# Weights in their second role: the values' halves stored 32 bytes further into their slots

## What is computed

```python
h = rmsnorm(x, g_pre)
u = h @ w_in                        # queries, keys, values, gates of three branches
o_a = latent attention              # first branch, 8 heads
o_b = differential attention        # second branch, 8 heads of value width 128
o_c = banded attention with bias    # third branch, 8 heads of value width 128
y = sum over n of gate_n * ((o_n * silu(z_n)) @ w_branch[n])
x = x + y @ w_out
```

## Time and profile before

| | |
|---|---|
| median of 3 runs | 3364.19 us (3363.44 to 3365.39) |
| the profiled execution's own time | 3364.12 us |
| its span (first to last instruction) | 3362.4 us |
| PE busy | 3319.8 us, 99% of the span |
| DVE busy | 2190.8 us, 65% |
| ACT busy | 1714.9 us, 51% |
| mean granted PE clock | 0.998 of full |

### The profile page before, as it was taken

One profiled execution on the slowest core, in us unless ns is written; L12 is line 12 of the kernel. 1 busy time (PEld: TensorE's weight loads), 2 busy tenths in 40 slices (PEclk: granted clock), 3 DMA queues, 4 the chain that ended last, 5 costly groups with the idle time before them and its releaser, 6 DMA issues. The chain is left out here.

```text
span 3362.4 us, 72952 instructions
## 1 busy us (share of the span) xinstructions
PE 3319.8 (99%) x27834; PEld 3279.7 (98%) x27834; DVE 2190.8 (65%) x3584; ACT 1714.9 (51%) x2803; POOL 309.7 (9%) x314
## 2 busy tenths in 40 slices
PE   7999999999999999999999999999999999999999
PEld 7999999999999999899999999999899999999999
DVE  7667666656656666678755665665778755666655
ACT  5555644434434455656544554444665654554443
POOL 1010100000000025011002200001012101210000
PEclk9999999999999999999999999999999999999999
DMA  5334455555555554344455545554444455445554
GB/s 187 109 112 148 176 185 190 188 187 186 190 186 188 186 189 163 135 163 163 156 203 184 180 163 188 187 198 177 148 151 164 155 178 206 173 163 188 188 206 163
DMA packets 90629, 584.28 MB, mean 174 GB/s; under 512 B 10480, under 2 KB 11120, under 8 KB 28400
## 3 DMA queue, kind: packets, MB, share of 16 engines
q1 hardware_dynamic: 88992, 577.47, 48.6%
q0 software_dynamic: 1488, 4.72, 0.4%
HBM read 580.05 MB, written 2.10 MB: 173 GB/s over the span
## 5 line engine op out<-in xcount | busy, mean ns | idle before, releaser
L174 DVE TENSOR_TENSOR w_lo<-raw,w_hi 128x768 fp32r<-128x768 f32 (+5 forms) x1202 | 1378.7, 1159 | 372.3 <-ACT w_hi L163 365.0
L193 PE MATMUL bank<-h,w_hi 128*128 128x256 f32 x5168 | 1459.2, 282 | 17.2 <-DVE w_lo L174 12.7
L163 ACT ACTIVATE w_hi<-raw 128x768 fp32r<-128x768 f32 (+4 forms) x1190 | 1096.8, 969 | 689.8 <-PE bank L195 614.6
L195 PE MATMUL bank<-h,w_lo 128*128 128x256 f32 x5168 | 1443.7, 279 | 0.0
L194 PE MATMUL bank<-h,w_hi 128*128 128x256 f32 x5168 | 1443.4, 279 | 0.0
L193 PEld LDWEIGHTS bank<-h,w_hi 128*128 128x128 f32 x5168 | 972.7, 188 | 22.8 <-DVE w_lo L174 10.8
L194 PEld LDWEIGHTS bank<-h,w_hi 128*128 128x128 f32 x5168 | 972.9, 188 | 2.6 <-issue 1.9
L195 PEld LDWEIGHTS bank<-h,w_lo 128*128 128x128 f32 x5168 | 972.5, 188 | 0.0
L193 PE MATMUL bank<-mixed,w_hi 128*128 128x256 f32 x2272 | 634.8, 279 | 0.7 <-DVE w_lo L174 0.7
L194 PE MATMUL bank<-mixed,w_hi 128*128 128x256 f32 x2272 | 634.1, 279 | 0.0
L195 PE MATMUL bank<-mixed,w_lo 128*128 128x256 f32 x2272 | 634.0, 279 | 0.0
(11 more groups left out here) (408 smaller groups left out, 3335.7 us busy)
## 6 DMA issues: line engine op xcount, KB each, us to landing
raw<-in_w SPq DMA_DIRECT2D x485, 1024.0 KB, 4.8
raw<-in_w_br SPq DMA_DIRECT2D x96, 512.0 KB, 3.9
raw<-in_w_uq SPq DMA_DIRECT2D x8, 768.0 KB, 4.4
raw<-in_w_ukv SPq DMA_DIRECT2D x8, 512.0 KB, 3.2
bias_t<-in_bias POOLq DMA_DIRECT2D x16, 192.0 KB, 4.2
x<-in_x SPq DMA_DIRECT2D x4, 512.0 KB, 8.3
raw<-in_w_kr SPq DMA_DIRECT2D x4, 512.0 KB, 3.3
out_x<-x SPq DMA_DIRECT2D x3, 512.0 KB, 7.5
```

What stands on the lines that cost most here:

```text
L163: act.activation(w_hi[:, b % 2, c], raw[:, b, c], ACT.Copy).then_inc(S["hi_done"], 1)
L174: dve.tensor_tensor(w_lo[:, b % 2, c], raw[:, b, c], w_hi[:, b % 2, c].bitcast(F32), ALU.subtract).then_inc(S["lo_done"], 1)
L193: pe.matmul(o, w_hi[:, b % 2, c], a_hi, start=start and k == t0, stop=False)
L195: last = pe.matmul(o, w_lo[:, b % 2, c], a_hi, start=False, stop=stop and k == t0 + nt - 1)
```

## The change

Both w_hi and w_lo get 16 more columns in all for each slot (2 x 8), so each slot is 64 bytes longer. For units 2 and 3 of a body with e = 0 in head_body, that is for the values' weights of the second and third branch, ACT and DVE write their halves 8 elements (32 bytes) further into the slot, and head_values reads them there. All other units are written and read from the slot's start. In head_body ACT now calls split_hi_part twice in place of split_hi once, and split_hi_part has both waits (raw_full and unit_done) before each part; DVE's two parts had their waits one by one before.

```diff
+TURNED = 8
...
-        w_hi = sb("w_hi", [2, UNIT], F32R)
-        w_lo = sb("w_lo", [2, UNIT], F32R)
+        w_hi = sb("w_hi", [2, UNIT + 2 * TURNED], F32R)
+        w_lo = sb("w_lo", [2, UNIT + 2 * TURNED], F32R)
...
+        def moved(c, at):
+            return slice(c.start + at, c.stop + at)
+
-        def split_hi_part(act, n, b, k, cols=UNIT):
+        def split_hi_part(act, n, b, k, cols=UNIT, at=0):
             at_least(act, f"raw_full{b}", 16 * n + 16)
             at_least(act, "unit_done", 4 * n + b - 1)
             c = parts(cols)[k]
-            act.activation(w_hi[:, b % 2, c], raw[:, b, c], ACT.Copy).then_inc(S["hi_done"], 1)
+            act.activation(w_hi[:, b % 2, moved(c, at)], raw[:, b, c], ACT.Copy).then_inc(S["hi_done"], 1)
...
-            dve.tensor_tensor(w_lo[:, b % 2, c], raw[:, b, c], w_hi[:, b % 2, c].bitcast(F32),
+            dve.tensor_tensor(w_lo[:, b % 2, moved(c, at)], raw[:, b, c], w_hi[:, b % 2, moved(c, at)].bitcast(F32),
...
+        def value_at(b, e):
+
+            return TURNED if e == 0 and b in (2, 3) else 0
...
-                    split_hi(act, n + (b + 1) // 4, (b + 1) % 4)
+                    for k in range(2):
+                        split_hi_part(act, n + (b + 1) // 4, (b + 1) % 4, k, at=value_at(b + 1, e))
...
-                    split_lo(dve, n + (b + 1) // 4, (b + 1) % 4)
+                    for k in range(2):
+                        split_lo_part(dve, n + (b + 1) // 4, (b + 1) % 4, k, at=value_at(b + 1, e))
...
-                    c = slice(2 * k * P, (2 * k + 2) * P)
+                    c = slice(TURNED + 2 * k * P, TURNED + (2 * k + 2) * P)
```

More of the change, by code:

```diff
@@ L168, in split_hi_part, with split_lo_part @@
             c = parts(cols)[k]
-            act.activation(w_hi[:, b % 2, c], raw[:, b, c], ACT.Copy).then_inc(S["hi_done"], 1)
-        def split_lo_part(dve, n, b, k, cols=UNIT):
+            act.activation(w_hi[:, b % 2, moved(c, at)], raw[:, b, c], ACT.Copy).then_inc(S["hi_done"], 1)
+        def split_lo_part(dve, n, b, k, cols=UNIT, at=0):
             c = parts(cols)[k]
             dve.wait_ge(S["hi_done"], 8 * n + 2 * b + k + 1)
-            dve.tensor_tensor(w_lo[:, b % 2, c], raw[:, b, c], w_hi[:, b % 2, c].bitcast(F32),
+            dve.tensor_tensor(w_lo[:, b % 2, moved(c, at)], raw[:, b, c], w_hi[:, b % 2, moved(c, at)].bitcast(F32),
                               ALU.subtract).then_inc(S["lo_done"], 1)
@@ L1531, in hybrid_layers @@
     sb, at_least, first_tiles = g["sb"], g["at_least"], g["first_tiles"]
-    load_unit, split_hi, split_lo, split_lo_part, unit, unit_tiles, of = (
-        g[k] for k in ("load_unit", "split_hi", "split_lo", "split_lo_part", "unit", "unit_tiles", "of"))
+    load_unit, split_hi, split_hi_part, split_lo, split_lo_part, unit, unit_tiles, of = (
+        g[k] for k in ("load_unit", "split_hi", "split_hi_part", "split_lo", "split_lo_part", "unit", "unit_tiles", "of"))
     x, h, ident, ones, ones64, eps, shared = (g[k] for k in ("x", "h", "ident", "ones", "ones64", "eps", "shared"))
```

## The result

The changed kernel takes 3402.03 us (median of 5, 3400.88 to 3403.47), the kernel before 3365.15 us (3363.44 to 3367.11) in the same comparison: ratio 1.011, 95% interval 1.0099 to 1.0121. It is 37 us slower. The forecast was 3361.5 us, and the range ended at 3371.7.

What follows compares the result with a forecast made beforehand. The prediction took PE's matmul pace as the bound: 3364.2 us less 2.7 for the moved reads, with moved writes, added waits and moved tensors at nothing, gave 3361.5 us. The range was 3358.1 to 3371.7 us.

Steps and rivals of the forecast that it cites:

- PE's pace is what counts, waits are not: Over the changed stretches PE is busy nearly throughout, so time can come only from the pace of its matmuls.
- The moved writes and the added waits: ACT and DVE splits of value units: extra time hidden by 4.9 us of slack, cost nothing; uncovered 0.8 and 26 us.
- The moved tensors: Slots 1 of w_hi and w_lo 64 past a multiple of 128, everything behind moved: nothing, if only place within 64 matters.
- The moved reads: 1536 value matmuls go from 118.4 to the ordinary pace of 116.7 ns, by the moving operand's place: 2.7 us less.
- rival 2: Value matmuls: both operands at the same place collide, 1.5 us more, 3365.7 us; at the upper end 3371.7; chance 0.11.
- Rival 1: Value matmuls: the stationary operand's place makes the 118.4 ns and stays, so nothing happens, 3364.2 us; chance 0.23.
- Rival 3: Longer slots 1 bring half the ordinary matmuls to their slower pace: 12.6 us more, 3374 us in all; chance 0.07.
- Rival 4: More than the forecast: values at 115 ns and layer 2's slow stretch back to 95.09 us, 3358.1 us; chance 0.05.

Runs made afterwards that it cites:

- its control: The kernel before with slots 512 bytes longer and the descriptor generator's scratch 2048 bytes smaller, values unshifted: 3364.74 us, ratio 0.9999.

## Why the prediction was wrong, step by step

- **PE's pace is what counts, waits are not:** right. The 37 us are pace alone, and PE's idle time even fell.
- **The moved writes and the added waits cost nothing:** right. The wait for w_lo stayed (13.0 us), and the shift with all places kept, added waits included, comes to 1.7 us over its control, no more than the 2.4 us that the value matmuls' pace accounts for.
- **The moved tensors, "I take nothing":** this step failed, and with it the sum. I put the term at nothing on the condition that only the place within 64 bytes matters, and had no row for that condition. The runs show that places within 256 bytes do. The longer slots put w_hi's slots at 128 and 192 and w_lo's at 0 and 64, h staying at 160: distances 32, 224, 160 and 96 in place of four times 32. w_lo by 128 alone costs 42.7 us, slots 1 by 64 alone 14.7 us, the layout of the change 39.6 us. Of these 39.6 the paces of the single distances give about 28: (2 x 116.77 + 118.08) / 3 in slot 0 and (2 x 118.33 + 119.97) / 3 in slot 1 is 118.04 ns on average, 1.27 over before, for 22225 matmuls. The rest is under "What stays open".
- **The moved reads, -2.7 us:** wrong in sign. I gave the pace to the moving operand's place; it belongs to the distance. The shift makes it 0 where the places are kept, and the values went to 119.89 ns, +2.4 us. That was my rival 2, with the row that I had set aside (L2553 at 282). In the changed kernel itself the longer slots spread the values over distances 0, 128, 64 and 192 and hid this: 117.8 ns, less than before, but so is the same layout without the shift, 118.0.
- **Rival 1, the stationary place alone:** wrong as well. With the values 64 bytes on, the stationary h kept its place and the pace fell to 116.72.
- **Rival 3, longer slots slow the ordinary units:** right in place and sign. Its mechanism, slots 1 at 64 past 128, was sized at 12.6 us and measured at 14.7. The nearness is partly luck: it took the second pace of distance 32, 117.8 ns, and slots 1 have the pace of distance 224 (in the long runs of that kernel the units alternate between 118.3 and 116.7 ns). What it lacked is that the longer w_hi also moves w_lo by 128, which costs more than the slots do. I gave it 7 in 100 because nothing before told 64 from 128. But nothing told them apart because all slots of the weights had one place within 256 bytes, and h and mixed another, which is no evidence for "nothing".
- **Rival 4:** not met. No steady pace of 115 was seen: the 115.36 ns at distance 192 is a mix of 113.3 to 113.5 and 117.8.

The Trainium skill, page "TensorE: Matmul & The Clock Gate", section "Step-by-step: what each phase is for", says of PE's two read ports that "Loading the next tile's weights doesn't steal SBUF read bandwidth from the running matmul." The traces speak against that for these fp32r matmuls: with the same instructions, 3.2 ns of 116.8 (2.7%) hang on where the one operand lies against the other. That it is the load that holds up the running matmul is argued from this and not shown, since no run here has such matmuls without a load for each. The Trainium skill's page "SBUF — State Buffer", section Specifications (TRN2), has lines of 16 bytes; steps of 32 bytes, two whole lines, moved the pace from 119.96 to 116.77 and on to 117.73, so the rule of whole lines, by which the prediction worked out no effect, does not hold here.

**What stays open.** Where w_hi and w_lo have different places the pace is not the mean over their distances, in either direction. With w_lo alone moved the ordinary matmuls have 118.84 ns where the mean of 32, 32 and 160 is 117.2, which would make some 10 of the 42.7 us; the value matmuls of the same run have 117.08 where the mean of 224, 224 and 96 is 118.9. So something between one load and the next counts too, and no run separates it; in the changed kernel about 12 of the 40 us hang on it. (With slots 1 moved, where each unit has one distance, the mean of 116.77 and 118.33 is 117.55, and 117.48 was measured.) Nor was it shown what chooses between the two paces of a distance; held at the fast one of distance 192 throughout, 22225 matmuls at 113.3 in place of 116.8 would by this estimate be worth some 78 us. Steps finer than 32 bytes were not tried, and that places repeat every 256 bytes was tested at the places of before alone.

## What to carry to other kernels

Before lengthening any buffer in a kernel that PE bounds, write down where each matmul operand will lie afterwards; a few bytes of padding move everything behind them, and that can cost more than the padded step is worth (here 39.6 us for a step forecast at 2.7). A pace that differs between two kinds of matmuls of one shape may be a relation between their operands until a run moves one of them alone. And when a layout is tuned, try the eight distances: a filler of some elements is the cheapest experiment there is, and here it was worth from +2.1% to -0.5%. Take more single times where they spread, and look at stretches of the trace: a mean can hide two paces.

## What the runs showed of the hardware

With fp32r matmuls of 128 x 256 back to back, each with its own load, at a granted clock of 0.998 of full, the distance of starts depends on the place of the moving operand less that of the stationary one. Moving h or w_lo by 256 bytes changed nothing (3363.68 and 3364.90 us against 3364.31), by 128 w_lo cost 42.7 us. The paces by distance, where all weights have one place:

- 0: 120.0 ns; 96: 120.0; 224: 118.3.
- 32: 116.7, with short stretches at 117.8.
- 64 and 192: 117.8 or 113.3.
- 128: 120.0 or 118.7; 160: 118.7 or 117.3.

Which operand is the weight and which the activation makes no difference to the mean at 0, 32, 96, 128, 160 and 224; at 64 and 192 both roles show the same two paces in other shares. The same instructions with the same operands can hold one of two paces for hundreds of matmuls.
